# Attention by pairs of query tiles: low parts of the keys in 64-row tiles, scaling of the probabilities on GpSimd, casts on VectorE

## The reference

```python
s = jnp.einsum('bdhnqc,bdhnkc->bdhnqk', qb, kw) * (HEAD_DIM ** -0.5) + bias   # per branch
m = jnp.max(s, -1, keepdims=True); p = jnp.exp(s - m); den = jnp.sum(p, -1, keepdims=True)
o = jnp.einsum('bdhnqk,bdhnkc->bdhnqc', p / den, vw); lse = (m + jnp.log(den))[..., 0]
# the branches (128,1), (512,4), (2048,16) are merged by softmax over lse
```

## Time and profile before

| | |
|---|---|
| median of 3 runs | 2756.37 us |
| profiled execution, first to last instruction | 2753.8 us (its own total isn't recorded apart from this span) |
| mean granted TensorE clock | 0.985 of full speed |
| busy PE / weight loads | 2655.6 us (96%) / 2077.3 us (75%) |
| busy DVE / ACT / POOL | 1855.0 (67%) / 1573.1 (57%) / 171.3 us (6%) |
| attention stage, about | 316 to 541 us |

### The profile page before, as it was taken

The page is one execution under the profiler, slowest core; times in us unless marked ns, Lnnn a source line. Parts: engine busy times, 40 slices in busy tenths (PEclk is TensorE's granted clock), DMA queues, the critical chain, the costliest instruction groups (busy, mean ns, idle before and its releaser), DMA issues.

```text
span 2753.8 us, 49497 instructions
## 1 busy us (share of the span) xinstructions
PE 2655.6 (96%) x20657; PEld 2077.3 (75%) x20657; DVE 1855.0 (67%) x2264; ACT 1573.1 (57%) x2010; POOL 171.3 (6%) x145
## 2 busy tenths in 40 slices
PE   8999899998499999999999999999999999999997
PEld 8898777786377777777777777777777777777765
DVE  4330389856777677766776766767766766776788
ACT  3102488722366566666666666666666666666663
POOL 0100000000000000100000010000001000000043
PEclk9999999999699999999999999999999999999999
DMA  5000111232587687878887787878887877878895
GB/s 185 31 32 16 45 44 41 81 113 103 211 315 278 252 311 284 297 287 285 290 314 275 270 297 280 306 276 288 294 303 284 297 277 265 311 283 278 297 340 217
DMA packets 293147, 636.87 MB, mean 231 GB/s; under 512 B 21971, under 2 KB 68435, under 8 KB 292883
## 3 DMA queue, kind: packets, MB, share of 16 engines
q1 hardware_dynamic: 282268, 601.31, 60.0%
q0 software_dynamic: 9024, 26.87, 3.5%
q10 hardware_dynamic: 1632, 5.51, 0.5%
HBM read 607.34 MB, written 26.28 MB: 230 GB/s over the span
## 4 chain that ended last, share of the span: by engine, by line
PE 92%; DVE 4%; ACT 2%; issue 1%; DMA 1%; POOL 0%; SPq 0%; DVEq 0%; POOLq 0%; ACTq 0%
PE banks L722 17%; PE banks L461 14%; PE banks L679 12%; PE banks L680 12%; PE banks L681 12%; PE banks L698 11%; PE banks L735 5%; PE banks L570 2%; PE banks L559 2%; PE banks L543 1%; PE banks L710 1%; DVE w_parts L1017 1%; ACT probs L855 1%; ACT probsT L849 1%; PE banks L650 0%
## 5 line engine op out<-in xcount | busy, mean ns | idle before, releaser
L1017 DVE TENSOR_TENSOR w_parts<-raw_units,w_parts 128x1024 fp32r<-128x1024 f32 x1056 | 1267.4, 1222 | 446.1 <-ACT w_parts L961 413.3
L961 ACT CAST w_parts<-raw_units 128x1024 fp32r<-128x1024 f32 x1056 | 1102.8, 1052 | 539.2 <-PE banks L681 252.1
L679 PE MATMUL banks<-w_parts,xs_parts 128*128 128x512 f32 x1408 | 564.0, 401 | 4.4 <-DVE w_parts L1017 4.0
L680 PE MATMUL banks<-w_parts,xs_parts 128*128 128x512 f32 x1408 | 551.4, 392 | 0.0
L681 PE MATMUL banks<-w_parts,xs_parts 128*128 128x512 f32 x1408 | 551.0, 391 | 0.0
L722 PE MATMUL banks<-w_parts,h_parts 128*128 128x512 f32 x2112 | 498.4, 394 | 0.7 <-DVE w_parts L1017 0.7
L722 PEld LDWEIGHTS banks<-w_parts,h_parts 128*128 128x128 f32 x2112 | 391.7, 188 | 90.6 <-issue 10.0
L679 PEld LDWEIGHTS banks<-w_parts,xs_parts 128*128 128x128 f32 x1408 | 265.6, 189 | 82.2 <-issue 25.1
L698 PE MATMUL banks<-raw_units,xs_short 128*32 128x256 f32 (+1 forms) x6144 | 317.5, 362 | 0.0
L681 PEld LDWEIGHTS banks<-w_parts,xs_parts 128*128 128x128 f32 x1408 | 265.4, 188 | 57.0
L680 PEld LDWEIGHTS banks<-w_parts,xs_parts 128*128 128x128 f32 x1408 | 265.8, 189 | 51.2
(11 more groups left out here) (185 smaller groups left out, 2120.2 us busy)
## 6 DMA issues: line engine op xcount, KB each, us to landing
raw_units<-in_w_gate SPq DMA_DIRECT2D x352, 512.0 KB, 8.8
raw_units<-in_w_up SPq DMA_DIRECT2D x352, 512.0 KB, 9.7
raw_units<-in_w_down SPq DMA_DIRECT2D x352, 512.0 KB, 8.0
win_raw<-in_w_in SPq DMA_DIRECT2D x10, 1024.0 KB, 5.5
relT<-rel_bias SPq DMA_DIRECT2D x8, 960.0 KB, 4.5
x_rows<-x SPq DMA_DIRECT2D x10, 512.0 KB, 2.7
acc_rows<-ax SPq DMA_DIRECT2D x10, 512.0 KB, 2.9
fin<-acc_rows POOLq DMA_DIRECT2D x10, 512.0 KB, 7.5
```

What stands on the lines that cost most here:

```text
L679: nc.tensor.matmul(out, xs_parts[:, HI, k, :], w_hi, start=k == 0, stop=False)
L680: nc.tensor.matmul(out, xs_parts[:, LO, k, :], w_hi, start=False, stop=False)
L961: nc.scalar.copy(w_parts[:, HI, n % SPLIT, :], raw[:, n % RING, :]).then_inc(s_hi, 1)
L1017: return nc.vector.tensor_tensor(out, whole, high.bitcast(F32), ALU.subtract)
```

## The change

Units are taken in pairs (NP = 40); a pair has the same head and group. `halves(h)` gives the head's own 64 rows (`here`) and the others (`there`).

- **Scores.** The high matmuls of both units stay as they are (128 rows). The low part of unit i of the pair is a matmul of 64 rows, rows 64i to 64i+63, so `k_low` now holds the same data in both halves, and `q_again` holds q's high part of every second tile in the other half. No zeros are needed. The low matmuls alternate between the two units.
- **Order on PE** in step p: scores of pair p, transposes of unit 2p-2, values of pair p-2 (all keys, one visit), transposes of unit 2p-1.
- **ACT** in step p: copy of 2p-2, exp of 2p, copy of 2p-1, exp of 2p+1. It casts for head 0 only (`first_high`).
- **DVE** in step p: bias of 2p, reciprocal of 2p-1, bias of 2p+1, reciprocal of 2p, casts for the next head (`HIGH_AT`: two in the first pair of a head, one in the second, one in the third), copies to `attT` of the pair p-2. Low parts only for head 0 (`first_low`).
- **GpSimd** in step p: scaling of unit 2p-1, scaling of unit 2p, then subtractions of 64x256 in place, ten per head (`REST_AT`: 2, 3, 3 and 2 in the second to fifth pair). The place of the rest is q's or k's own tile.
- **SP**, per head and piece: five DMAs from `here` to `there` (`copy_parts`; one of them, of `k_low`, to `here`), each behind the cast or subtraction that makes its data. The first pair of a head and group waits for all five (`s_dup`). `relT` and `w_out` come behind them in SP's queue.

The diff, cut ("..." where lines are left out):

```diff
+        q_again = [place(f"q_again{i}", at, P * TILES // 2, dt=F32R) for i, at in enumerate((19712, 32000))]
...
+        HIGH_STEPS = [(what, piece) for piece in range(2) for what in ("k", "q")]
+        HIGH_AT = {0: (0, 1), 1: (2,), 2: (3,)}
+        REST_AT = {1: (0, 1), 2: (2, 3, 4), 3: (5, 6, 7), 4: (8, 9)}
+        REST_STEPS = [(what, c) for what, c in (("q", 0), ("k", 0))] + \
+                     [(what, c) for what in ("k", "q") for c in range(L_PROMPT, TOKENS, L_PROMPT)]
+        REST_OF_PIECE = [{"q": 1, "k": 2}, {"k": 6, "q": 10}]
...
+            def copy_parts(h, piece):
+                here, there = halves(h)
...
+                sp.wait_ge(s_kq, len(HIGH_STEPS) * (h - 1) + HIGH_STEPS.index(("k", piece)) + 1)
+                sp.dma_start(k_high[there, slot, cols].bitcast(F32), k_high[here, slot, cols].bitcast(F32)).then_inc(done, 16)
+                sp.wait_ge(s_kq, len(HIGH_STEPS) * (h - 1) + HIGH_STEPS.index(("q", piece)) + 1)
+                sp.dma_start(by_tiles(q_again[slot][there, :].bitcast(F32))[:, first:first + n, :],
+                             by_tiles(q_parts[here, slot, :].bitcast(F32))[:, tiles, :]).then_inc(done, 16)
+                for what in REST_OF_PIECE[piece]:
+                    sp.wait_ge(s_rest, len(REST_STEPS) * (h - 1) + REST_OF_PIECE[piece][what])
+                    if what == "q":
+                        sp.dma_start(q_parts[there, slot, cols].bitcast(F32), q_tile(h // 2)[here, cols]).then_inc(done, 16)
+                    else:
+                        for half in (here, there):
+                            sp.dma_start(k_low[half, slot, cols].bitcast(F32), kT[here, h // 2, cols]).then_inc(done, 16)
+            for h in range(1, HEADS):
+                for piece in range(2):
+                    copy_parts(h, piece)
+                if h + 1 < HEADS:
+                    load_relT(h + 1)
...
+            def scores(p):
...
+                        pe.wait_ge(s_dup[h % 2][g], PARTS_IN * ((h + 1) // 2))
+                for i in range(2):
+                    if p >= 1:
+                        pe.wait_ge(s_scored, 2 * p - 1 + i)
+                    qs = t0 + units[2 * p + i][2] * P
+                    for c in range(0, glen[g], 512):
+                        nc.tensor.matmul(psum[:, 2 * i + c // 512, 0:cn], q_parts[:, h % 2, qs:qs + P], k_high[:, h % 2, t0 + c:t0 + c + cn],
+                                         start=True, stop=False)
+                for c in range(0, glen[g], 512):
+                    for i in range(2):
+                        half, tile = slice(HD * i, HD * i + HD), gtile[g] + units[2 * p + i][2]
+                        q = q_parts[half, h % 2, tile * P:(tile + 1) * P] if i == h % 2 else \
+                            q_again[h % 2][half, tile // 2 * P:(tile // 2 + 1) * P]
+                        last = nc.tensor.matmul(psum[:, 2 * i + c // 512, 0:cn], q, k_low[half, h % 2, t0 + c:t0 + c + cn],
+                                                start=False, stop=True)
+                last.then_inc(s_qk, 2)
...
+            for p in range(NP + 2):
+                if p < NP:
+                    scores(p)
+                if 1 <= p <= NP:
+                    turn_probs(2 * p - 2)
+                if p >= 2:
+                    values(p - 2)
+                if 1 <= p <= NP:
+                    turn_probs(2 * p - 1)
...
+            def first_high(piece):
...
+                nc.scalar.copy(k_high[here, 0, cols], kT[here, 0, cols]).then_inc(s_sh, 1)
+                nc.scalar.copy(q_parts[here, 0, cols], q_tile(0)[here, cols]).then_inc(s_sh, 1)
+                nc.scalar.copy(k_high[there, 0, cols], kT[here, 0, cols]).then_inc(s_sh, 1)
...
+            def first_low(piece):
...
+                low(k_low[here, 0, cols], kT[here, 0, cols], k_high[here, 0, cols]).then_inc(s_sl, 1)
...
+                low(q_parts[there, 0, cols], q_tile(0)[here, cols], q_parts[here, 0, cols]).then_inc(s_sl, 1)
+                low(k_low[there, 0, cols], kT[here, 0, cols], k_high[here, 0, cols]).then_inc(s_sl, 1)
...
+            def reciprocal_den(m):
+                dve.wait_ge(s_probs, m + 1)
+                if m >= 2:
+                    dve.wait_ge(s_soft, m - 1)
+                nc.vector.reciprocal(rden[:, m % 2:m % 2 + 1], den[:, m % 8:m % 8 + 1]).then_inc(s_rden, 1)
...
+                nc.vector.tensor_copy((q_parts if what == "q" else k_high)[here, h % 2, cols], src).then_inc(s_kq, 1)
...
-            nc.vector.memset(k_low[HD:P, 0, :].bitcast(F32), 0.0)
-            link(nc.vector.memset(k_low[0:HD, 1, :].bitcast(F32), 0.0))
...
-                    nc.vector.tensor_scalar(pr, pr, rden[:, m % 2:m % 2 + 1], None, ALU.mult).then_inc(s_soft, 1)
...
+            def take_high_away(h, step, norms):
...
+                pool.wait_ge(s_kq, len(HIGH_STEPS) * (h - 1) + HIGH_STEPS.index((what, int(c0 > 0))) + 1)
+                pool.wait_ge(s_soft, norms)
...
+                nc.gpsimd.tensor_tensor(whole, whole, high.bitcast(F32), ALU.subtract).then_inc(s_rest, 1)
...
+            def normalise_probs(m):
+                pr = probs[m % 4][:, 0:glen[units[m][1]]]
+                pool.wait_ge(s_rden, m + 1)
+                if rest_before(m):
+                    pool.wait_ge(s_rest, rest_before(m))
+                nc.gpsimd.tensor_scalar(pr, pr, rden[:, m % 2:m % 2 + 1], None, ALU.mult).then_inc(s_soft, 1)
...
+            for p in range(NP + 1):
...
+                if p >= 1:
+                    normalise_probs(2 * p - 1)
+                if p < NP:
+                    normalise_probs(2 * p)
+                if h + 1 < HEADS:
+                    for step in REST_AT.get(i, ()):
+                        take_high_away(h + 1, step, min(2 * p + 1, NU))
```

More of the change, by code:

```diff
@@ L530, in _ @@
                 pe.wait_ge(s_free[eng], sum(e == eng for _, _, e in jobs))
[L531 to L572, removed]
@@ new lines, in turn_probs, with values @@
+            def turn_probs(m):
+                pe.wait_ge(s_soft, m + 1)
+                if m >= 1:
+                    pe.wait_ge(s_ptc, m)
+                for kt in range(glen[units[m][1]] // P):
+                    last = nc.tensor.transpose(psum[:, 4 + kt // 4, kt % 4 * P:(kt % 4 + 1) * P],
+                                               probs[m % 4][:, kt * P:(kt + 1) * P], ident)
+                last.then_inc(s_pt, 1)
+            def values(r):
+                h, g, _ = units[2 * r]
+                nk = glen[g] // P
+                pe.wait_ge(s_ptc, 2 * r + 2)
+                if r >= 2:
+                    pe.wait_ge(s_att, 2 * r - 2)
+                for kt in range(nk):
+                    for i in range(2):
+                        last = nc.tensor.matmul(psum[HD * i:HD * i + HD, 6 + r % 2, 0:P],
+                                                v_rows[:, gtile[g] + kt, h * HD:(h + 1) * HD], probsT[(2 * r + i) % 4][:, kt, :],
+                                                start=kt == 0, stop=kt == nk - 1)
+                last.then_inc(s_pv, 2)
@@ L859, in cat_copy @@
+            for piece in range(2):
+                first_high(piece)
+            for p in range(NP + 1):
+                if p >= 1:
+                    probs_copy(2 * p - 2)
+                if p < NP:
+                    exponent(2 * p)
+                if p >= 1:
+                    probs_copy(2 * p - 1)
+                if p < NP:
+                    exponent(2 * p + 1)
             def cat_copy(t):
@@ L1090, in _, with attended @@
+            def attended(m):
+                h, g, qt = units[m]
+                t0 = (gtile[g] + qt) * P
+                dve.wait_ge(s_pv, m // 2 * 2 + 2)
+                nc.vector.tensor_copy(attT[HD * (h % 2):HD * (h % 2) + HD, h // 2, t0:t0 + P],
+                                      psum[HD * (m % 2):HD * (m % 2) + HD, 6 + m // 2 % 2, 0:P]).then_inc(s_att, 1)
             dve.wait_ge(s_job, len(jobs))
-            nc.vector.memset(k_low[HD:P, 0, :].bitcast(F32), 0.0)
-            link(nc.vector.memset(k_low[0:HD, 1, :].bitcast(F32), 0.0))
+            for piece in range(2):
+                first_low(piece)
```

181 lines of the change are left out of this document (99 added, 82 removed).

## The result

The kernel after takes **2844.31 us** in the median of 4 runs (2843.61 to 2844.61), the kernel before 2756.48 beside it: ratio 1.0314, 95% interval 1.0302 to 1.0326. It is 88 us slower. The forecast was 2749.2 (2740 to 2768) with 0.46 on faster: wrong in sign and far outside the range. The profiled execution spans 2842.6 us.

A forecast was written before the change was run, and what follows sets the result against it. PE was taken to bound attention, busy 25.8 of 26.77 us per head. New heads: 24.5 + 0.94 + 0.1 + 0.25 = 25.8; eight times -0.97, -0.25, +0.8 for the ends gave -7.2: 2749.2 us, range 2740 to 2768.

The forecast's parts named there:

- T: Duration of POOL's scaling of 1024 columns: put between 1.07 and 1.70 us, 1.07 taken.
- Rival 1: POOL's scaling is slow, at the affine_select's rate (1.70 us), so PE waits: +2.4 us per head, 2768 us; chance 0.20.
- POOL's sum: GpSimd's work per head, scalings plus subtractions: 18 us, fitting if in time.
- Tiles: Low score matmuls of 64 rows run two by two: 1.81 us less per head, each visit costing 0.50 us of switching.
- A visit to the values: PE's switch to the values' 64-column tiles and back: 0.42 us each, five visits per head instead of ten.
- Rival 2: The low tiles don't run side by side, so 1.81 us per head stays: +12 us, 2761 us; chance 0.08.
- A steady sample pair: PE's time from one sample pair's scores end to the next: 5.65 us.
- The late place in the third pair: PE reaches the transposes early behind the short prompt values and waits for POOL's scaling: 0.94 us once a head.
- The DMA stall: A head's first sample scores wait for the copy behind POOL's last subtractions: 0.25 us, to 0.65 with slower landing.
- Ends: Attention stage's start +0.5 us (first sample scores at 322.7 instead of 322.23) and its end +0.3 us.
- Rival 3: DVE's casts hold POOL up through shared SBUF access: +1.0 us per head, 2757 us, no change; chance 0.20.
- DVE and ACT no bound: Per head DVE sums to 18.5 us and ACT to 8 x 2.25 + 1.9 = 19.9, against PE's 24.5.

The follow-up runs named there:

- run 6: Kernel after, with GpSimd scaling only the first half of each unit's columns, the rest left unscaled: 2771.23 us, ratio 1.0056 to the kernel before.
- run 2: Kernel after, with the scaling back on DVE and the later heads' casts moved from DVE to ACT: 2751.58 us, ratio 0.9977 to the kernel before.
- run 9: From run 2, the low matmuls have 128 rows again instead of 64, in the same pairs: 2756.70 us, ratio 1.0005 to the kernel before.
- run 1: Kernel after, with the scaling back on DVE and only the subtractions left on POOL: 2752.56 us, ratio 0.9992 to the kernel before.
- run 3: Kernel after, with the later heads' casts moved from DVE to ACT and the scaling still on POOL: 2839.44 us in a single execution.
- run 4: Kernel after, with POOL scaling by a constant in place of the reciprocal read from memory: 2839.54 us in a single execution.
- run 5: Kernel after, with POOL's scaling as a tensor_tensor, the reciprocal broadcast along the row, instead of a tensor_scalar: 2785.41 us in a single execution.

## Why the prediction was wrong

**The step that failed is T**, in the part on the other engines: "So T, the scaling of 1024 columns, is between 1.07 and 1.70 us. I take 1.07". Measured: 2.84 us undisturbed, 2.94 in the mean. The two ends were rates of other instructions, a memset (0.83 ns a column) and an affine_select (1.45). They were treated as bounds, and the lower one was taken with the reason "one read, one write, no index arithmetic", and nothing in the trace supported that. The tensor_scalar itself costs (2.85 - 0.93) / 768 = **2.5 ns a column** and 0.29 fixed: three times the memset's rate. The only row of the same operation, at 128x1, gave the fixed part well (0.22) and said nothing on the rate.

**Rival 1 had the mechanism**: PE waiting for POOL in most pairs, through the loop scores, bias, reciprocal, scaling, transposes. The working had it "free while T is below 1.45", and the rival 2768 at T = 1.70; run 6 put T at 1.66 and the time at 2771.2. With the true T, the working by what the kernel after shows would have been: sample pairs at the higher of 4.25 + T = 7.1 and, where POOL has three subtractions, 2T + 3 x 0.73 + 0.25 = 8.1, in place of 5.65. The rival had the loop alone; that POOL's own sum could pass PE's was in no case. The chance of 0.20, too, came from the false bound: above 1.70 no case stood.

Point by point, for the rest:

- *POOL's sum, 18 us.* 32.5 a head. The subtractions were right: 0.73 us each, 0.8 taken. The estimate of 0.77 from the Trainium skill (GPSIMD Engine Reference, Performance versus the Vector engine) agrees with it.
- *Tiles.* They run two by two, as said: two low matmuls start at 423.78 and two at 424.12 in run 2. By the prediction's way of counting, the visit costs 0.48 us (0.50 predicted). A visit to the values in the same pair costs (425.46 - 424.44 - 0.853) + (427.36 - 425.46 - 1.706) = 0.17 + 0.19 = 0.36 us (0.42 predicted). Rival 2 is out. What was mis-sized is the 128-row matmul: 0.213 us was taken, run 9 shows 1.93 / 8 = 0.24, so the tiles are worth more than stated. That the total came out right (1.76 us against 0.853 + 0.427 + 0.50 = 1.78) is in part luck: the visit itself is nearer 0.32, and the matmuls are longer.
- *A steady sample pair.* 5.53 us in run 2 (422.68 to 428.21) against 3.2 + 2.45 = 5.65 in the working.
- *The late place in the third pair*, "0.94 us, once a head": PE waits 1.1 us there in run 1, 0.6 in run 2.
- *Missed*: in a head's first pair the scores are short, and PE reaches the transposes before ACT's copy is out of the banks: 0.64 us at 403.15 in run 2, once a head. This and the late places stand in a head of 26.1 us, against 25.8 worked out.
- *The DMA stall*, 0.25 us expected: once in the trace of run 2, 0.41 us at 407.55, `q_parts`. The copies of 256 KB land after 2.9 to 3.3 us where 2.5 to 2.9 had been taken.
- *Ends.* The first sample scores start at 322.61 (322.7 predicted).
- *Rival 3, contention with DVE*: it exists. It was put at 1.0 us a head, 8 us; in this kernel it costs about 6 (run 3), through scalings of up to 3.34 us and casts of up to 1.57, beside a far longer T than assumed.
- *DVE and ACT no bound*: right; they have 15.8 to 19.1 us of 38.

With the scaling left on DVE the plan gives 2752.6 or, with the casts on ACT, 2751.6 us, 2 to 3 us above the forecast of 2749.2. That is near, but it is another kernel; what the kernel after would take with T = 1.07 no run shows. DVE has room for the scaling (in run 2 it is busy for 41.7 of 52.6 us and ends few waits of PE), so there was little for the move to gain. Why the tensor_scalar is slower on this engine than the tensor_tensor stays open; the runs show only that the operand (run 4) and DVE (run 3) are not the reason.

## What to carry to other kernels

Rates of other instructions don't bound an instruction that the trace has never shown wide: if the forecast hangs on it, widen the range until it would change the verdict, and say at which duration it does. An engine that is idle is not a free place for a step on the loop that ends in the next start of the bottleneck: ask for the step's latency there, not for its share of the engine. An order that brings dependent steps closer together (one pair in place of three tiles between scores and transposes) can save switches on the bottleneck and raises the price of each late step: the same slow scaling cost 10 us in the old order and 92 in the new, 56 of them still there when GpSimd had nothing else to do.

## What the runs showed of the hardware that was not expected

- **GpSimd's tensor_scalar is slower than its tensor_tensor**, on the same data. In the means of the kernel after and of run 5, 128x1024 fp32 takes 2.94 us against 1.99 and 128x256 takes 0.99 against 0.64, so 2.5 and 1.8 ns a column. With a constant (run 4) the 1024 columns take 2.87. DVE takes 0.754.
- **DVE's casts and GpSimd's scalings hold each other up, mostly by waiting.** In the kernel after, the two engines' timelines, each instruction by itself:

```profile
411.45 2.84 POOL L1510 TENSOR_SCALAR probs<-probs,rden 128x1024 f32<-128x1024 f32 x1 [0.17 <-POOL kT L1498]
413.37 1.46 DVE L1188 CAST q_parts<-qT_first 64x1024 fp32r<-64x1024 f32 x1
414.27 3.27 POOL L1510 TENSOR_SCALAR probs<-probs,rden 128x1024 f32<-128x1024 f32 x1
```

  A cast of 1024 columns takes 0.67 us where nothing holds it. This one began 1.9 us into a scaling that kept its 2.84 us, and ended at 414.83, 0.54 behind that scaling's end; the next scaling took 3.27. In the whole stage nine casts began 1.82 us or more into a scaling. All nine ended 0.54 us (1024 columns) or 0.14 us (256 columns) behind its end, whenever they had begun, so they waited for it. Five others began 1.50 to 1.72 us into one and were not held; in the three of 1024 columns (0.67 us each) it was the scaling that took longer, 3.27 or 3.28 us. (The other fourteen casts began less than 0.2 us before or after a scaling did, and none was held.) The Trainium skill (SBUF — State Buffer, Who interferes with whom) has the shared pair as an exclusive lock for the whole instruction. The nine agree with it; the three that passed in the middle of a scaling don't, and speak for a lock held for less than an instruction. Which it is stays open.
- **A 512-column matmul with a fresh weight load passes every 0.24 us** in a row of eight (run 9, 1.93 us at a granted clock of 1.00), and not every 0.213.
- **TensorE's clock, at 2.4 GHz in the heads before (1.00, rows 2), fell to 1.2 GHz in parts of the stage after**: 0.50 was granted from 411.00 to 416.30 and 0.53 behind the 2.30 us of waiting that end at 431.00, and 1.00 in the stretch ahead of that, which holds a wait of 1.49. In run 6, with heads of 28.8 us, it was 1.00 over the four heads.
